# Modulation matmuls in four column strips with deferred row sums, and rotary query loads queued ahead of the second half's stores

## The reference

```python
for l in range(DEPTH):                       # 4 layers, D = 2048
    mod = cs @ w_mod[l] + b_mod[l]           # cs = silu(c), one row; w_mod[l] is 2048 x 6144
    shift, scale, gate = split(mod, 3)
    h = rmsnorm(x, g_pre[l]) * (1 + scale) + shift
    y = mla_band_mixer(h, ...) if l % 2 == 0 else spatial_gating_mixer(h, ...)
    x = x + gate * rmsnorm(y, g_post[l])
# in the even mixer: q = concat(q_nope, rope(q_rope)), k = concat(k_nope, rope(kr) shared by the heads)
#   oa = softmax(q k^T / sqrt(192)) v under a chunk-causal mask; ob = banded attention with a bias table
#   y = concat(oa, ob) * silu(gate_path) @ w_out
```

## Time and profile before

| | |
|---|---|
| median of 3 runs | 5430.91 us (5397.25 to 5671.55) |
| the profiled execution, its own time | 5386.55 us |
| its span on the slowest core (core 2) | 5385.0 us |
| spans of the 8 cores | 5339.5 to 5385.0 us |
| PE busy | 4820.4 us (90%) |
| DVE, ACT, POOL busy | 1592.6, 1397.6, 783.0 us |
| start, norms and first projections | 0 to 445 us |
| attention of layer 0, A heads then B heads | 445 to 942, 942 to 1604 us |
| attention of layer 2, A heads then B heads | 3040 to 3535, 3535 to 4190 us |

### The profile page before, as it was taken

The page is one execution under the profiler, slowest core; times in us unless marked ns, Lnnn a source line. Parts: engine busy times, 40 slices in busy tenths (PEclk is TensorE's granted clock), DMA queues, the critical chain, the costliest instruction groups (busy, mean ns, idle before and its releaser), DMA issues.

```text
span 5385.0 us, 68490 instructions; the slowest of 8 cores (5339.5 to 5385.0 us)
## 1 busy us (share of the span) xinstructions
PE 4820.4 (90%) x25572; PEld 2207.7 (41%) x25572; DVE 1592.6 (30%) x2640; ACT 1397.6 (26%) x2507; POOL 783.0 (15%) x722
## 2 busy tenths in 40 slices
PE   4188989989889999999899899899988999999999
PEld 0033333455544433444344333345555444444444
DVE  0233222223234422111253433212333452211123
ACT  0212333333343212000132144333334331200011
POOL 1530000000002201222233100000000230022200
PEclk6599999999989998999999999999999999999999
DMA  9631222232346735442574212222333765322143
GB/s 169 169 65 40 48 48 34 48 59 51 58 99 180 173 60 87 79 79 48 140 195 98 51 30 48 42 48 51 64 59 67 178 178 99 63 40 40 33 146 142
DMA packets 233348, 458.45 MB, mean 85 GB/s; under 512 B 145744, under 2 KB 150544, under 8 KB 212544
## 3 DMA queue, kind: packets, MB, share of 16 engines
q0 software_dynamic: 66912, 239.63, 25.8%
q1 hardware_dynamic: 166112, 214.45, 13.7%
HBM read 588.57 MB, written 71.50 MB: 123 GB/s over the span
## 4 chain that ended last, share of the span: by engine, by line
PE 79%; DMA 8%; DVE 4%; ACT 4%; issue 2%; POOL 2%; SPq 0%; DVEq 0%; ACTq 0%; POOLq 0%
PE PS L363 79%; DMA woo_163<-sg_w_out 1%; DMA WB_54<-w_mod 1%; ACT ua_86 L373 1%; DMA R_44<-hb_60 1%; ACT ua_87 L373 1%; DVE PS L382 1%; DMA WB_54<-sg_v 1%; DVE ua_87 L382 1%; DMA RAW<-rowst_124 1%; DMA WB_51<-sg_ug 1%; DMA xto_141<-x 1%; POOL hb_59 L385 1%; DMA WB_55<-sg_ug 0%; DVE ua_86 L382 0%
## 5 line engine op out<-in xcount | busy, mean ns | idle before, releaser
L363 PE MATMUL PS<-R_43,WB_47 128*128 128x512 bf16 x1024 | 249.7, 380 | 0.0
L363 PE MATMUL PS<-R_43,WB_51 128*128 128x512 bf16 x896 | 213.9, 380 | 0.7 <-DVE v_76 L388 0.7
L363 PE MATMUL PS<-R_43,WB_49 128*128 128x512 bf16 x896 | 213.9, 380 | 0.0
L391 DVE RECIPROCAL st<-st 128x1 f32<-128x1 f32 x160 | 26.2, 163 | 634.5 <-ACT st L373 634.5
L363 PE MATMUL PS<-R_43,pf 128*128 128x512 bf16 x512 | 118.6, 394 | 82.2 <-DMA R_43<-hb_60 82.2
L363 PE MATMUL PS<-q_73,k_75 128*128 128x512 bf16 (+3 forms) x544 | 185.9, 342 | 0.0
L363 PE MATMUL PS<-q_72,k_74 128*128 128x512 bf16 (+3 forms) x544 | 179.3, 330 | 0.0
L377 DVE TENSOR_SCALAR R_44<-PS 128x512 bf16<-128x512 f32 x128 | 88.5, 691 | 241.9 <-PE PS L363 240.9
L363 PE MATMUL PS<-R_43,WB_52 128*128 128x512 bf16 x640 | 159.8, 392 | 0.0
L363 PE MATMUL PS<-R_43,WB_48 128*128 128x512 bf16 x640 | 157.2, 386 | 0.0
L382 DVE SCALAR_TENSOR_TENSOR tv_69<-PS,lng_t,E 128x512 f32<-128x512 f32 x64 | 48.0, 750 | 360.4 <-PE PS L363 360.4
(11 more groups left out here) (461 smaller groups left out, 9475.8 us busy)
## 6 DMA issues: line engine op xcount, KB each, us to landing
XA<-xte_147 SPq DMA_DIRECT2D x16, 1024.0 KB
XA<-xte_148 SPq DMA_DIRECT2D x16, 1024.0 KB
xto_141<-XA SPq DMA_DIRECT2D x16, 1024.0 KB
xto_142<-XA SPq DMA_DIRECT2D x16, 1024.0 KB
WB_47<-w_mod POOLq DMA_DIRECT2D x25, 512.0 KB, 6.9
WB_48<-w_mod POOLq DMA_DIRECT2D x25, 512.0 KB, 8.4
WB_49<-w_mod POOLq DMA_DIRECT2D x25, 512.0 KB, 10.4
WB_50<-w_mod POOLq DMA_DIRECT2D x25, 512.0 KB, 8.2
```

The source lines that it names most:

```text
L363: P.op("pe", lambda e: e.matmul(o, lhsT, rhs, start=start, stop=stop), r=r, w=w, sig=sig)
L391: P.op("dve", lambda e: e.reciprocal(o, i), r=r, w=w, wp=wp)
```

## The change

Five edits. (1) A modulation step writes 32 rows of the bank: `csT` holds each column 32 times, step k works on ring buffer k % 4 and writes partitions 32j to 32j+31 with j = k % 4, so four partial rows are left, which must be added. (2) DVE copies the whole bank, SP stores four partial rows, `mod_final` only issues the loads, and the sums and the store of `ROW` are put on a list `final` that is emptied at the end of the next modulation group, at `first_norm` or at the start of `out_phase`. There is one `rowst` instead of two. (3) A modulation step costs 1 on the queue instead of 4. (4) The loads of the first rotary queries stand after the first half's stores, and a rotary block pumps an eleventh of the queue instead of an eighth. (5) exp(-gate) in `ua` is issued at the first tile of a query group instead of the last.

```diff
-    RAW = dscr("RAW", [4, 6144], F32)
+    RAW = dscr("RAW", [4, 3, 4, D], F32)
...
-        rowst = [cb("rowst%d" % i, 512, F32, 1) for i in range(2)]
-        fin = [cb("fin%d" % i, 128, F32, 16) for i in range(3)]
+        rowst = cb("rowst", 512, F32)
+        fin = [cb("fin0", 512, F32, 16)] + [cb("fin%d" % i, 128, F32, 16) for i in (1, 2)]
...
-            act(csT[:], ccol_t[:], AF.Silu, r=[c_t], wp=[c_t])
+            act(csT[:].rearrange("p (k m) -> p k m", m=32), ccol_t[:].unsqueeze(2).to_broadcast([128, 16, 32]), AF.Silu, r=[c_t], wp=[c_t])
...
-                mm(bank(b)[0:1, :], csT[:, kc:kc + 1], w_, kc == 0, kc == 15, r=[wt, c_t], w=[PS_t[b]], sig=(kc == 15))
-                if kc == 15:
+                j, kk = k % 4, k // 4
+                kc = 4 * j + kk
+                w_, wt = wkc(s_["p"], kc)
+                mm(bank(b)[32 * j:32 * j + 32, :], csT[:, kc * 32:(kc + 1) * 32], w_, kk == 0, kk == 3, r=[wt, c_t], w=[PS_t[b]], sig=(k == 15))
+                if k == 15:
                     done(jobs_of(s_["p"]))
-                    rs_ = rowst[cg % 2]
-                    cp("dve", rs_[:], bank(b)[0:1, :], r=[PS_t[b]], w=rs_.t())
-                    dma("sp", RAW[l:l + 1, cg * 512:(cg + 1) * 512], rs_[:], r=rs_.t(), wp=[RAW_t[l][cg // 4]])
+                    flush_final()
+                    rs_ = rowst
+                    cp("dve", rs_[:], bank(b), r=[PS_t[b]], w=rs_.t())
+                    for q in range(4):
+                        dma("sp", RAW[l, cg // 4, q, (cg % 4) * 512:(cg % 4 + 1) * 512], rs_[32 * q:32 * q + 1, :], r=rs_.t(), wp=[RAW_t[l][cg // 4]])
...
-            return [(4, lambda kc=kc: step(kc)) for kc in range(16)]
+            return [(1, lambda k=k: step(k)) for k in range(16)]
...
-            tt("dve", fin[0][:], fin[0][:], fin[1][:], ALU.add, r=[ft[0], ft[1]], w=ft[0])
...
+            def rest():
+                tt("dve", fin[0][:, 0:256], fin[0][:, 0:256], fin[0][:, 256:512], ALU.add, r=[ft[0]], w=ft[0])
+                o = fin[0][:, 0:128]
+                tt("dve", o, o, fin[0][:, 128:256], ALU.add, r=[ft[0]], w=ft[0])
+                tt("dve", o, o, fin[1][:], ALU.add, r=[ft[0], ft[1]], w=ft[0])
                 if k == 1:
...
+                dma("sp", ROW[l, k, :].rearrange("(p c) -> p c", c=128), o, r=[ft[0]], w=[ROW_t[l][k]])
+
+            final.append(rest)
...
         def out_phase(l, yr, wb, N_, Xprev, Xnext, last, pf_src):
 
+            flush_final()
             rep_load(N_.rep[0], l, 2)
...
-            each = total_cost() / 8.0
+            each = total_cost() / 11.0
...
+                if gr == 0:
+                    head_loads(0)
+                    head_loads(2)
             done(jr[1])
             drain()
-            head_loads(0)
-            head_loads(2)
...
-                if last:
-                    ti = cnt["u"] % 2
-                    cnt["u"] += 1
-                    gs, gt_ = yslot(hd, g)
-                    a_, b_ = ua[ti], ub[ti]
+                ti = (4 * hd + g) % 2
+                gs, gt_ = yslot(hd, g)
+                a_, b_ = ua[ti], ub[ti]
+                if idx == 0:
                     act(a_[:], gs, AF.Exp, r=gt_, w=a_.t(), scale=-1.0)
```

More of the change, by code:

```diff
@@ L318, in build @@
         onesf = cb("onesf", 128, F32)
-        csT = cb("csT", 16, BF16)
+        csT = cb("csT", 16 * 32, BF16)
         ccol_t = cb("ccol_t", 16, F32)
@@ L488, in consts, with step @@
             dma("sp", lnb_t[:], lnb_col[:, :], wp=[c_t])
-            act(csT[:], ccol_t[:], AF.Silu, r=[c_t], wp=[c_t])
+            act(csT[:].rearrange("p (k m) -> p k m", m=32), ccol_t[:].unsqueeze(2).to_broadcast([128, 16, 32]), AF.Silu, r=[c_t], wp=[c_t])
         def mod_units(l, cg, banks):
             s_ = {}
-            def step(kc):
-                if kc == 0:
+            def step(k):
+                if k == 0:
                     s_["p"] = pieces(w_mod[l, cg])
@@ L514, in mod_group, with flush_final @@
                 fn()
+        final = []
+        def flush_final():
+            while final:
+                final.pop(0)()
         def mod_final(l, k):
             ft = [fin[j].t() for j in range(3)]
-            dma("sp", fin[0][:], RAW[l, k * 2048:(k + 1) * 2048].rearrange("(p c) -> p c", c=128), r=[RAW_t[l][k]], w=ft[0])
+            f3 = fin[0][:].rearrange("p (j c) -> p j c", c=128)
+            dma("sp", f3, RAW[l, k].rearrange("j (p c) -> p j c", c=128), r=[RAW_t[l][k]], w=ft[0])
             dma("sp", fin[1][:], b_mod[l, k * 2048:(k + 1) * 2048].rearrange("(p c) -> p c", c=128), w=ft[1])
-            tt("dve", fin[0][:], fin[0][:], fin[1][:], ALU.add, r=[ft[0], ft[1]], w=ft[0])
             if k > 0:
@@ L523, in mod_final @@
                 dma("sp", fin[2][:], g[l, :].rearrange("(p c) -> p c", c=128), w=ft[2])
-                if k == 1:
[L525 to L528, removed]
+            def rest():
[3 more added lines that the diff above has]
+                tt("dve", o, o, fin[1][:], ALU.add, r=[ft[0], ft[1]], w=ft[0])
+                if k == 1:
+                    stt("dve", o, o, 1.0, fin[2][:], ALU.add, ALU.mult, r=[ft[0], ft[2]], w=ft[0])
+                elif k == 2:
+                    tt("dve", o, o, fin[2][:], ALU.mult, r=[ft[0], ft[2]], w=ft[0])
+                dma("sp", ROW[l, k, :].rearrange("(p c) -> p c", c=128), o, r=[ft[0]], w=[ROW_t[l][k]])
+            final.append(rest)
         def rep_load(b, l, which):
```

1 line of the change is left out of this document (removed).

## The result

The changed kernel takes 5188.42 us (median of 4, 5182.10 to 5797.11), the kernel before in the same series 5414.08 us (median of 4, 5392.03 to 5671.55). The forecast was 5205 us, and the result lies inside the range of 5155 to 5290. The profiled execution took 5182.10 us against 5386.55 before, 204.5 us less, where the sum said 199.

What follows compares the result with a forecast made beforehand. TensorE, busy 90% of the span, was taken as the bound. 68 + 35 + 66 + 36 - 4 - 2 = 199 us off the profiled 5386.55 leaves 5188, scaled by 0.35% to 5205 us; range 5155 to 5290.

Steps and rivals of the forecast that it cites:

- 1. Deferred sums: Even layers' heads: six long TensorE waits behind DVE's stalled sums vanish, with the low clock after them; 68 us.
- 2. Rotary queries: Even layers' first score matmuls: earlier loads remove 29.4 us of waits and 7.5 us of clock loss; 35 us.
- the 2 us for the rotary loop: Even layers' rotary loop: 2 us taken off because the loop follows DVE more closely.
- 3. Strips: Modulation groups: four strips side by side shorten them, 60 us in the heads and 6 us in odd layers.
- a wrong limit: Modulation groups: weight loads one after the other, 0.075 us each, set the pace; 2.8 and 2.2 us saved a group.
- the upper bound's 4 x 0.215: Modulation groups: four strips in the time of one matmul, 0.9 us, 1.2 us in total a group.
- 4. exp(-gate): Ends of query groups: with `ua` ready early, DVE starts 2.0 us sooner; half of 73.0 us of waits, 36 us.
- 5. Elsewhere: Losses: even layers' output phases late by 2 us each (22 us of cover left), 4 in all; start 2 us.
- rival (d): Output phases: late row and residual loads, beyond 22 us of cover, slow the kernel to about 5515 us; chance 0.02.
- (a): Modulation groups: strips run in series, so the sum loses 59 us, giving 5265 us; chance 0.18.
- (b): DVE sums: the round trip still stops DVE, through the one `rowst` or SP, giving 5273 us; chance 0.07.
- (c): Early exponential gives nothing, as TensorE waits for DVE's two operations or a score exponential; 5241 us; chance 0.08.

Runs made afterwards that it cites:

- the repeated execution: The changed kernel run again with no edit, beside the third set of runs: 5179.99 and 5191.44 us, ratio to before 0.9623.

## Why the prediction was right

Undoing the parts one by one on the changed kernel costs 57 (strips) + 14 (cost on the queue) + 47 (exponential) + 20 to 28 (rotary), and the sums alone were worth 64 in the heads of the kernel before: 202 to 210 us, where the whole change brought 204.5. That fits better than the parts are known. In the heads alone, over the eight cores, the undone parts make 51 + 14 + 57 + 5 and 77 for the sums (100 less the 23 of the longer round trip), 204 us, and the whole change gained 184 there. So the parts act in different waits and add up, as the sum took for granted, but only to about a tenth.

**1. Deferred sums, 68.** Right: 64 in the heads of the kernel before, some 73 in those of the changed one. The clock in them is 14 and 10 us by TensorE's busy time, for the 11 reckoned. The six waits are gone, and the sums stand 1.8 us ahead of a copy, as allowed. Missed was what the four stores do to a round trip (23 us in six); it is hidden now, and matters only when the sums are done at once.

**2. Rotary queries, 35.** The mechanism is right, and the load went out 2.6 us after the time reckoned (413.6 for 411). The size was off: the stages gained 12.0 and 10.0, and the clock behind the waits some 4 (the heads of the kernel with the old loads are that much longer), together 26. The term that failed is the 2 us for the rotary loop: without the waits of 16.5 and 12.9 us the stages would be 256.4 and 171.1 us, and they are 260.8 and 174.0, so the loop lost 4.4 + 2.9 = 7.3. The run with an eighth puts about 5 of it on the eleventh.

**3. Strips, 60 + 6.** The sum is right, in the heads to 2 us, by a wrong limit. `csT` fell by 61.5 us in the heads (26.50 + 22.80 to 9.91 + 8.45 in layer 0, much the same in layer 2). The odd layers gained 8.9 by stage on the slowest core and 3.6 over the eight cores, for the 6 reckoned: `csT` fell by 41.6 us there, and waits for modulation weights took 29.6 of it back, as the prediction had it. But the weight loads are not what holds a group in the heads: four strips start within 0.01 us, where loads one after the other would have put them 0.075 apart. By the upper bound's 4 x 0.215 a group would cost 1.2; the rest is the changes to the heads' matmuls, and the wait for the bank, which no step had. The Trainium skill's rule in "TensorE: Matmul & The Clock Gate", section "The mechanism", that loads overlap only where the row group differs, does not hold for these strips: they share all rows and start together, and the next four loads begin at 758.34 and 758.35, while matmuls of 758.33 still run. Its figure of 2.38 for three strips, in "Measured speedup vs the span model", gave 1.4 us; the two runs of steps take 0.60 + 0.83 = 1.4 where no bank is waited for, so the figure came near, though there are four strips here and it is for three.

**4. exp(-gate), 36.** Too low: 47 by the times, 57 by the heads. "About half of the wait" was read from one place; over both layers `ua` fell by 46 of 73 us, less 13 that score exponentials now wait. What was left out is the clock, which part 1 had counted behind its stalls: stalls of up to 3.9 us go with a lower one too (0.98 and 0.97 in the B heads without part 4, 0.99 in both with it), and it makes the 17 us of busy time above.

**5. Elsewhere, -4 and -2.** The sizes are about right, the places are not. The output phases lost 5.8, but 4.2 of it in the odd layers, for which the prediction had nothing, and -0.1 and 1.7 in the even ones, for which it had 2 each. The start lost 2.8 (1.1 in the repeated execution), and the first norm ends 4.2 later (2.8). The row loads of layer 0, beside the earlier trace rows:

```profile
1500.61 0.69 DVE L385 TENSOR_TENSOR R_44<-ub_89,ua_87 128x512 bf16<-128x512 f32 x1 [1.01 <-ACT ua_87 L373]
1501.22 0.79 DVE L385 TENSOR_TENSOR fin_124<-fin_124 16x256 f32<-16x256 f32 x2
...
1503.47 0.33 SPq L397 DMA_DIRECT2D repe_143<-ROW  x1
...
1526.39 2.36 DVE L382 SCALAR_TENSOR_TENSOR PS<-PS,st,repe_143 128x2048 f32<-128x2048 f32 x1
```

The first use comes 25.8 us after the last gate product, 25.7 before. In layer 2 it comes 27.0 us after it, 25.7 before, which is past the 26 us that the prediction had set; but DVE waited there for ACT's `st` of the norm, not for the row, whose load was issued 24 us earlier. The 22 us of cover held, and rival (d) had little to stand on. (One figure in it is off: 5515 is 1.5% above the 5430.91 from which the prediction takes its 2%; 5540 would be 2%. Nothing else uses it.)

**The rivals.** (a) is out: in series the kernel takes 5244, and the changed kernel does not. (b) is out in the heads, where no copy waits for stores or round trip. Its mechanism is there elsewhere: four copies wait 2.3 to 8.5 us for the stores of the group ahead through the one `rowst`, one at the start and three in layer 1, and three sums wait 8.8 to 15.7 us for the round trip, two at the start and one in layer 1. Beside the longest of these copies TensorE waits 7.8 and 3.0 us for modulation weights, as in the earlier trace rows. (c) is out as a whole, though its mechanism is there with 13 us. Of the 17 us between 5205 and 5188, 6 are in the sum and the rest is the scaling to the median shown; three executions of the changed kernel lie within 5182 to 5190.

One thing that helped was on no list: the cost of 1 changed the pace of the queue. With a cost of 4 again, 15 us of waits for `q` and `v` come back; from the kernel before to the changed one they fell from 22.9 us in 32 to 13.3 in 6. With part 4's 11 this more than fills the 9 that part 2 lacks.

## What to carry to other kernels

Where a small matmul has one or a few output rows, give it 32 columns and put the parts of its contraction in four column strips: four then cost about one, and the gain is the matmul's own time times three quarters, but only where TensorE and not the weights is waited for. Work that must wait for a trip through memory belongs one work item later in its engine's order, and the price of leaving it in place grew here when the trip went from one row to four (58.3 to 81.5 us in six trips). After taking a wait away, read the list of waits again for what is left: here a bank chosen by a counter, waited for before the change too, and weights asked for three groups at a time, were together worth half as much as the whole change.

## What the runs showed of the hardware

Column strips run side by side whether the program deals them out in turn (eleven steps in 0.76 us: 758.33 to 759.09) or strip by strip (0.99 us), against 2.48 in one strip; in the second order eleven steps of three strips start in threes, some 0.22 us apart. Three strips in a run cost as much as one: 0.33 and 0.30 us up to the next matmul, where the cost is 4. Weight loads of 128 x 32 do not set the pace: eight of them begin within 0.02 us (758.33 to 758.35). In one kernel six cores ran layer 0's output phase at a mean granted clock of 0.86 or 0.87, with 160 us at 0.81, a level between the two of 1.2 and 2.4 GHz; in the traces of the other kernels this phase has a mean of 0.97 to 0.99. It cost some 30 us, and its cause is open.
